# Gates of a hybrid decoder layer: block products in place of plain tiles for ten of twelve pairs of column tiles

## The reference, cut to what matters

```python
gates = jax.nn.sigmoid((h @ w_gate[l] + b_gate[l]).astype(jnp.float32))
gates = gates.astype(x.dtype).reshape(b, s, N_BRANCH, D_MODEL)
merged = (gates[:, :, 0] * (o_a @ w_o_a[l])
          + gates[:, :, 1] * (o_b @ w_o_b[l])
          + gates[:, :, 2] * (o_m @ w_o_m[l]))
x = x + merged @ w_out[l]
x = x + conv_ffn(rmsnorm(x, ffn_norm[l]), w_up[l], conv_w[l], conv_b[l], w_down[l])
```

## Time and profile before

| | |
|---|---|
| time, median of three runs | 1750.19 us (1750.15 to 1750.33) |
| time of the profiled execution | 1753.89 us, of which 1752.1 us are its span |
| PE matmul busy | 1681.4 us (96%) |
| DVE, ACT, POOL busy | 848.1, 634.4, 865.3 us |
| gates stage on PE | 591.05 to 857.29 us of the span |
| output projections | 857.29 to 969.3 us |

### The profile page before, as it was taken

One profiled execution on the slowest core, in us unless ns is written; L12 is line 12 of the kernel. 1 busy time (PEld: TensorE's weight loads), 2 busy tenths in 40 slices (PEclk: granted clock), 3 DMA queues, 4 the chain that ended last, 5 costly groups with the idle time before them and its releaser, 6 DMA issues.

```text
span 1752.1 us, 22400 instructions
## 1 busy us (share of the span) xinstructions
PE 1681.4 (96%) x8625; PEld 1381.5 (79%) x8625; DVE 848.1 (48%) x1242; ACT 634.4 (36%) x1135; POOL 865.3 (49%) x671
## 2 busy tenths in 40 slices
PE   5999999999899899999999999899999999999999
PEld 4887878778677688888888787788888888788887
DVE  6555243457874112200155247788888888522101
ACT  5455565545544222222111323434343334322110
POOL 6543656533322122222144566999999998222221
PEclk9999999999999799999999999999999999999999
DMA  6113011110110233332355711222232223443411
GB/s 214 37 58 100 1 37 40 37 45 13 43 37 1 61 111 97 96 97 84 116 166 165 247 51 48 90 79 73 84 95 74 73 84 101 164 144 132 144 48 60
DMA packets 131253, 151.05 MB, mean 86 GB/s; under 512 B 16780, under 2 KB 97356, under 8 KB 131148
## 3 DMA queue, kind: packets, MB, share of 16 engines
q1 hardware_dynamic: 131148, 149.63, 26.9%
HBM read 116.98 MB, written 32.62 MB: 85 GB/s over the span
## 4 chain that ended last, share of the span: by engine, by line
PE 61%; DVE 2%; POOL 2%; DMA 1%; ACT 1%; issue 0%; SPq 0%; DVEq 0%; ACTq 0%; POOLq 0%
PE ps L2341 23%; PE ps L1694 15%; PE ps L2426 13%; PE ps L1710 6%; PE ps L1726 3%; DMA w_raw<-in_w_out_dram 1%; POOL wo L1587 1%; POOL f_lo L2182 0%; PE ps L1719 0%; DVE ffn_area L2299 0%; DVE attn_lo L2291 0%; DVE t_all L2209 0%; ACT wo L1518 0%; DVE ffn_area L1679 0%; DVE attn_out L2244 0%
## 5 line engine op out<-in xcount | busy, mean ns | idle before, releaser
L2182 POOL TENSOR_TENSOR f_lo<-ffn_area,f_hi 128x1024 fp32r<-128x1024 f32 x85 | 201.8, 2394 | 20.5 <-ACT f_hi L2069 20.5
L2341 PE MATMUL ps<-t_all,f_hi 128*128 128x512 f32 x528 | 164.1, 392 | 2.0 <-DVE t_all L2209 1.6
L1592 POOL TENSOR_TENSOR g_lo<-g_raw,g_hi 128x1024 fp32r<-128x1024 f32 x23 | 55.3, 2406 | 208.5 <-ACT g_hi L1502 208.5
L1694 PE MATMUL ps<-act_hi,g_hi 128*128 128x512 f32 x384 | 152.4, 397 | 3.4 <-DVE g_lo L1627 3.4
L2214 POOL TENSOR_TENSOR attn_lo<-ffn_area,attn_lo 128x512 fp32r<-128x512 f32 x44 | 58.6, 1331 | 194.3 <-ACT attn_lo L2131 194.3
L1694 PE MATMUL ps<-act_hi,g_lo 128*128 128x512 f32 x384 | 151.3, 394 | 0.0
L1694 PE MATMUL ps<-act_lo,g_hi 128*128 128x512 f32 x384 | 150.0, 391 | 0.0
L2069 ACT ACTIVATE f_hi<-ffn_area 128x1024 fp32r<-128x1024 f32 x85 | 80.2, 946 | 187.9 <-PE ps L2341 177.5
L2341 PE MATMUL ps<-act_hi,f_hi 128*128 128x512 f32 x336 | 133.1, 396 | 4.6 <-POOL f_lo L2182 4.6
L2341 PE MATMUL ps<-act_hi,f_lo 128*128 128x512 f32 x336 | 132.5, 394 | 0.0
L1229 PE MATMUL ps<-w_hi,act_hi 128*128 128x512 f32 (+1 forms) x320 | 123.0, 384 | 9.2 <-DVE act_lo L476 4.1
(11 more groups left out here) (258 smaller groups left out, 4257.8 us busy)
## 6 DMA issues: line engine op xcount, KB each, us to landing
ffn_area<-in_w_up_dram SPq DMA_DIRECT2D x44, 512.0 KB, 5.2
gates<-gate SPq DMA_DIRECT2D x24, 512.0 KB, 3.1
gate<-gates SPq DMA_DIRECT2D x24, 512.0 KB, 3.9
g_raw<-in_w_gate_dram SPq DMA_DIRECT2D x23, 512.0 KB, 4.6
z<-attn_out SPq DMA_DIRECT2D x22, 512.0 KB, 2.6
ffn_area<-in_w_down_dram SPq DMA_DIRECT2D x22, 512.0 KB, 4.2
ffn_area<-z SPq DMA_DIRECT2D x44, 256.0 KB, 3.0
attn_out<-in_x_dram SPq DMA_DIRECT2D x16, 512.0 KB, 6.0
```

The source lines that it names most:

```text
L1592: pool.tensor_tensor(g_lo[:, n % 3], g_raw[:, n % 2], g_hi[:, n % 3].bitcast(F32), ALU.subtract).then_inc(g_lo_done, 1)
L1694: ins = pe.matmul(ps[:, u % 4, :], w[:, n % 3, k, :], a[:, k, HALF[half]], start=(k == 0 and i == 0), stop=(k == NK - 1 and i == 2))
L2182: pool.tensor_tensor(part_place(p, part, f_lo, first_lo), part_source(p, part), part_place(p, part, f_hi, first_hi).bitcast(F32), ALU.subt ...
L2341: ins = pe.matmul(out, w, a, start=(start and k == 0 and i == 0), stop=(stop and k == 3 and i == 2))
```

## The change

- Column tiles `p` and `p + 12` form pair `p`. Pairs 0 and 1 stay plain (four tiles, 192 matmuls); pairs 2 to 11 are made by seven block products each (840 matmuls).
- The combined activations `T1` to `T4` are made during the plain tiles: DVE makes ten sums of 2048 elements (`difference`) and four low parts (`t_low`, `t4_low`), ACT four casts. `T4` replaces a block of `act_hi`/`act_lo` after the last plain tile.
- The weights go through the feed-forward's buffers: four raw tiles, `f_hi`/`f_lo` of seven slots, with casts on ACT, sums and low parts on POOL.
- Each pair's four quarters of 128 x 512 are summed by DVE into `staged[:, 0:2]`, put through the sigmoid in place by ACT and stored by 256 KB transfers (48 with those of the plain tiles, instead of 24 of 512 KB).
- The attention rows are no longer split in tiles 3 to 12 but in pair 11, the last, since `attn_hi` now shares memory with `t_all`. That pair takes its products in the order P5, P6, P7, P1, P2, P4, P3. The first products of the output projections wait for the rows and for the quarter sums that free their PSUM banks.
- The `w_o` weights of the first tile are loaded during pair 10 into a raw tile of their own; those of the second tile wait for the last sum. The first four casts of `w_out` wait for the end of the gates, not for the output projections.

The core of the diff, with the order of work on ACT, POOL, DVE and PE:

```diff
-WO_SLOT = [1, 2, 7, 8, 9, 10, 3, 4, 5, 6, 11, 12, 13, 14, 15, 0]
+WO_SLOT = [1, 2, 3, 4, 8, 9, 14, 15, 10, 11, 12, 13, 5, 6, 7, 0]
+GATE_AT = (1, 0, 2)
+SPLIT_ROWS = (0, 1, 2, 3, 6, 7, 8, 9, 4, 5)
+SPLIT_NEEDED = (2, 8, 10)
...
+GATE_PAIRS, PLAIN = 12, 2
+LAST_GATES = GATE_PAIRS - 1
+PLAIN_TILES = [(p, e) for p in range(PLAIN) for e in range(2)]
+PLAIN_SLOT = (A11, S3, S1, S3)
...
+def gate_products(p):
+
+    if p == PLAIN:
+        return P1, P2, P6, P5, P7, P4, P3
+    if p == LAST_GATES:
+        return P5, P6, P7, P1, P2, P4, P3
+    return tuple(range(7))
...
+GATE_CASTS = ([(0, 1), (1, 0), (2, "A1"), (1, 1), (2, "A22"), (2, "S12"), (2, "S34")] +
+              [(p, part) for p in range(PLAIN + 1, GATE_PAIRS) for part in ("S12", "A1", "A22", "S34")])
...
+            if n < 4:
+                eng.wait_ge(p_done, len(GATE_ORDER))
+            else:
+                eng.wait_ge(out_summed, UN * (NK - 1) + (2 if n < 6 else 4 if n < 8 else UN))
...
+            load_gate(0)
+            store_quarter(LAST_GATES, C22)
+            store_quarter(LAST_GATES, C11)
+            load_gate(1)
+            store_quarter(LAST_GATES, C21)
+            load_gate(2)
+            store_quarter(LAST_GATES, C12)
             load_o_weights(1)
...
+            cast(0, 1)
+            cast(1, 0)
             act.wait_ge(vectors_in, 32)
-            for n in range(NG):
-                f, b = n // BR, n % BR
-                for half in range(2):
-                    u = 2 * n + half
-                    if half == 0 and f >= 1:
-                        act.wait_ge(gate_out[b], 16 * f)
-                    act.wait_ge(gate_summed, u + 1)
-                    column = b * NK + f
-                    act.activation(gate[:, b, HALF[half]], ps[:, u % 4, :], ACT.Sigmoid,
-                                   bias=bias[:, column:column + 1]).then_inc(gate_done, 1)
-                if n + 3 < NG:
-                    cast_gate_weights(n + 3)
-                if SPLIT_FROM <= n < SPLIT_FROM + AT:
-                    i = n - SPLIT_FROM
-                    act.activation(attn_hi[:, i, :], attn_out[:, i, :], ACT.Copy).then_inc(attn_hi_done, 1)
-                if n >= NG - BR:
-                    cast_o_weights(0, n - (NG - BR))
+            plain_gate(0, 0, 0)
+            t_high(0)
+            plain_gate(0, 0, 1)
+            cast(2, "A1")
+            plain_gate(0, 1, 0)
+            t_high(1)
+            plain_gate(0, 1, 1)
+            cast(1, 1)
+            cast(2, "A22")
+            plain_gate(1, 0, 0)
+            plain_gate(1, 0, 1)
+            cast(2, "S12")
+            t_high(2)
+            plain_gate(1, 1, 0)
+            plain_gate(1, 1, 1)
+            t4_high()
+            for p in range(PLAIN, LAST_GATES):
+                cast(p, "S34")
+                if p > PLAIN:
+                    quarter_gate(p - 1, C12)
+                first_copy(p)
+                cast(p + 1, "S12")
+                quarter_gate(p, C11)
+                cast(p + 1, "A1")
+                quarter_gate(p, C22)
+                cast(p + 1, "A22")
+                quarter_gate(p, C21)
+            cast(LAST_GATES, "S34")
+            quarter_gate(LAST_GATES - 1, C12)
+            for i in range(6):
+                split_row(i)
+            cast_o_weights(0, 0)
+            for i in range(6, 8):
+                split_row(i)
+            first_copy(LAST_GATES)
+            for b in range(1, BR):
+                cast_o_weights(0, b)
+            for i in range(8, AT):
+                split_row(i)
+            for n in (C22, C11, C21, C12):
+                quarter_gate(LAST_GATES, n)
...
+            low(0, 1)
+            low(1, 0)
+            low(2, "A1")
+            add_weights(2)
+            low(1, 1)
+            low(2, "A22")
+            low(2, "S12")
+            for p in range(PLAIN, GATE_PAIRS):
+                low(p, "S34")
+                if p < LAST_GATES:
+                    add_weights(p + 1)
+                    for part in ("S12", "A1", "A22"):
+                        low(p + 1, part)
...
-            for i in range(AT):
...
+            def t1_made():
+                (a_hi, a_lo), (b_hi, b_lo) = block_of(0, 1), block_of(0, 0)
+                difference(1, t_raw[:, 0, 1], a_hi.bitcast(F32), b_hi.bitcast(F32))
+                difference(2, t_raw[:, 0, 0], a_lo.bitcast(F32), b_lo.bitcast(F32))
+                dve.wait_ge(comb_made, 2)
+                difference(3, t_raw[:, 0, 1], t_raw[:, 0, 1], t_raw[:, 0, 0], ALU.add)
...
+            def t_low(j):
+                dve.wait_ge(comb_hi, j + 1)
+                if j < 2:
+                    dve.wait_ge(comb_made, (4, 6)[j])
+                dve.tensor_tensor(t_all[:, j, 1], t_raw[:, j, 1], t_all[:, j, 0].bitcast(F32), ALU.subtract).then_inc(comb_lo, 1)
...
+            t1_made()
+            t2_made()
+            t_low(0)
+            t4_made()
+            t_low(1)
+            t3_made()
+            t_low(2)
+            t4_low()
+            for p in range(PLAIN, LAST_GATES):
+                if p > PLAIN:
+                    c12_sum(p - 1)
+                    u2_sum(p)
+                    c11_sum(p)
+                else:
+                    c11_sum(p)
+                    u2_sum(p)
+                u3_u4_sums(p)
+                c22_sum(p)
+                c21_sum(p)
+            c12_sum(LAST_GATES - 1)
+            for i in range(8):
+                split_low(i)
+            u2_sum(LAST_GATES)
+            u3_u4_sums(LAST_GATES)
+            c22_sum(LAST_GATES)
+            c11_sum(LAST_GATES)
+            for i in range(8, AT):
+                split_low(i)
+            c21_sum(LAST_GATES)
+            c12_sum(LAST_GATES)
...
+            def block_product(p, i, slot, hi, lo):
+                gate_bank_free(p, i)
+                for k in range(4):
+                    cols = slice(k * P, k * P + P)
+                    for m, (w, a) in enumerate(((f_hi, hi), (f_hi, lo), (f_lo, hi))):
+                        ins = pe.matmul(gate_bank(p, i), w[:, slot, cols], a[:, k, :], start=(k == 0 and m == 0),
+                                        stop=(k == 3 and m == 2))
+                ins.then_inc(p_done, 1)
...
+            for p in range(PLAIN, GATE_PAIRS):
+                for i in gate_products(p):
+                    pe.wait_ge(w_lo_done, gate_cast(p, PART_OF[i]))
+                    if i in COMBINED:
+                        j = COMBINED[i]
+                        if p == PLAIN:
+                            pe.wait_ge(comb_lo, j + 1)
+                        block_product(p, i, SLOT_OF[i], t_all[:, j, 0], t_all[:, j, 1])
+                    else:
+                        if p == PLAIN and i == P4:
+                            pe.wait_ge(comb_lo, 4)
+                        block_product(p, i, SLOT_OF[i], *block_of(*BLOCK_OF[i]))
...
+                    if f == 0:
+                        pe.wait_ge(attn_lo_done, SPLIT_NEEDED[b])
...
+                        elif at < 3:
+                            pe.wait_ge(summed, gate_sum(LAST_GATES, (C11, C21, C12)[at]))
```

More of the change, by code:

```diff
@@ new lines, in gate_sums @@
+def gate_sums(p):
+    if p == PLAIN:
+        return C11, U2, U3, U4, C22, C21, C12
+    if p == LAST_GATES:
+        return U2, U3, U4, C22, C11, C21, C12
+    return U2, C11, U3, U4, C22, C21, C12
+GATE_ORDER = ([(t, h) for t in PLAIN_TILES for h in range(2)] +
+              [(p, i) for p in range(PLAIN, GATE_PAIRS) for i in gate_products(p)])
+GATE_SUMS = [(p, n) for p in range(PLAIN, GATE_PAIRS) for n in gate_sums(p)]
+GATE_CASTS = ([(0, 1), (1, 0), (2, "A1"), (1, 1), (2, "A22"), (2, "S12"), (2, "S34")] +
+              [(p, part) for p in range(PLAIN + 1, GATE_PAIRS) for part in ("S12", "A1", "A22", "S34")])
@@ new lines, in part_place, with gate_bank, quarter, o_source @@
+        def part_place(p, part, w):
+            if part in (0, 1):
+                a = PLAIN_SLOT[PLAIN_TILES.index((p, part))]
+                b = a + 1
+            else:
+                a, b = PLACE[part]
+            return w[:, a:b + 1, :].rearrange("p a n -> p (a n)")
+        def gate_bank(p, i):
+            return ps[:, gate_product(p, i) % 8, :]
+        def quarter(n):
+            e, half = divmod(GATE_STORES.index(n), 2)
+            return quarters[:, e, HALF[half]]
+        def o_source(f):
+            return o_first if f == 0 else o_raw
@@ new lines, in u2_sum, with c11_sum @@
+            def u2_sum(p):
+                dve.wait_ge(copied, p - PLAIN + 1)
+                product_done(p, P6)
+                if p == PLAIN:
+                    dve.wait_ge(gate_out[3], 16 * PLAIN)
+                dve.tensor_tensor(u2, gate_bank(p, P6), s1(p), ALU.add).then_inc(summed, 1)
+            def c11_sum(p):
+                dve.wait_ge(copied, p - PLAIN + 1)
+                product_done(p, P2)
+                quarter_free(p, C11)
+                dve.tensor_tensor(quarter(C11), gate_bank(p, P2), s1(p), ALU.add).then_inc(summed, 1)
```

(30 more changed lines are left out.)

359 lines of the change are left out of this document (263 added, 96 removed).

## The result

The changed kernel takes **1723.42 us** (median of four runs, 1718.7 to 1724.15) against 1750.17 before: a ratio of 0.985, 95% interval 0.9837 to 0.9864, so 24 to 28.5 us less. A second comparison in five rounds gave 1720.33 against 1748.26, 0.9836 (0.9822 to 0.9849). The forecast was 1724.5 us, 25.7 less.

What follows compares the result with a forecast made beforehand. PE's matmul count was taken to bound the stage. Terms: −26.9 on PE, +0.6 and +0.6 us for two stalls, so −25.7 from the median 1750.2 gives 1724.5 us; range for 8 in 10, 1722.6 to 1730.

Steps and rivals of the forecast that it cites:

- PE alone: Gates: 20 plain tiles go (219.7 us), ten pairs of seven products come (192.8 us), a gain of 26.9 us.
- No waits in the steady pairs: Pairs 3 to 11: no stalls, with POOL at 13.7 us of work in a pair of 19.28 us.
- The A1 part: Tightest supply in the steady pairs: its low part ends near 16.1 us, the next pair begins at 19.3.
- The plain tiles: DVE and POOL queue in turns: pair 1's second tile gets its low part at 35.4 us plus about 0.1, against 35.6.
- POOL's third operation: Plain tiles: must be ready before 15.5 us or DVE gets in one operation more; its cast ends at 15.2, margin 0.2.
- a turn lost: Rival: one DVE operation more ahead of pair 1's second-tile low part adds 2.14 us, two 4.3: 1726.0 to 1730; chance 0.20.
- the 0.6: Stall of PE at the second tile of pair 1, taken as 0.6 us with 0 and 2.2 as ends.
- when PE wants the part: Second tile of pair 1: low part needed when six halves are done, 35.6 us after the first matmul.
- DVE's operation of 2048: Plain tiles: 2.29 us by the skill's formula, 2.14 us by the rows with turns, which the sum used.
- The hand-over: Last pair to output projections: PE waits 0.6 us for sum C21, ends 0 and 3; late rival 1727 to 1737, chance 0.06.
- every row meeting POOL: Last pair: ten DVE low parts each 1.44 us longer would make the stall about 12 us.
- `w_out` and the feed-forward stages: Behind the last pair: looser waits of the first `w_out` casts give nothing; everything later moves by the same amount.

Runs made afterwards that it cites:

- thin products: Changed kernel with 9 of 12 matmuls left out of P7, then of P7 and P3, in pairs 3 to 10: ten pairs 177.1 us, then 167.7 us.
- the variants: Five edits of the changed kernel with its code up to the pairs; with its own three traces, eight traces, low part ready at 35.45 or 37.63 us.
- old `w_out` waits: Changed kernel with the casts of `w_out` waiting as in the kernel before: the `w_out` stretch took 109.3 us, as with the new waits.
- C21 first: Changed kernel with DVE making sums C21 and C12 ahead of the last attention row's low part: pairs 192.6 us, no PE wait entering the output projections.
- P7 thin: Changed kernel with 9 of the 12 matmuls of P7 left out in pairs 3 to 10: ten pairs 177.1 us, no PE wait in them.

## Why the prediction was right, and where it was off

- **PE alone:** 26.9 us forecast. The ten pairs took 192.6 against 192.8 forecast; putting 120 matmuls back costs 27.2. Right, and the reason is shown.
- **No waits in the steady pairs:** right. The A1 part was forecast ready at 16.1 us; the thin products put the supply's pace at 16.3. The margin of 3.2 us was right to 0.2.
- **The plain tiles:** the sum of ten DVE and eight POOL holds put the low part at 35.4 us after the first matmul, plus 0.1, or one turn of 2.14 later. PE got it at 35.45 and at 37.63: both values were right to 0.1. The place where the turn is lost was the second one named, POOL's third operation, wanted before 15.5 us; the border lay at 15.42. So the rival "a turn lost" is what the profiled run did, and it happened in two of three traces of this kernel, three of eight with the variants. It was given 0.20. The time still fell into the forecast, since the forecast allowed both stalls up to 2 us together; the 0.6 itself was a mean of two ends, and none of the eight traces shows it.
- **What I had missed there:** when PE wants the part was put at 35.6 us, from one trace. It was 34.4 to 35.9, mostly by how long the clock stays at the lower level at the start, 2.9 to 5.7 us in these traces. So a third outcome came that two ends, 0 and 2.2, leave out: with the turn won and a short stretch, three runs (old `w_out` waits, C21 first, P7 thin) still waited 0.8 to 0.9 us.
- **DVE's operation of 2048:** 2.28 us alone, in line with the 2.29 of the Trainium skill (VectorE: DVE Perf Modes, section "The TRN2 errata — SBUF-src ops pay a fixed extra latency per instruction"). In turns it holds the port for about 2.1 to 2.2, since part of its length overlaps with POOL's. The turns were the right measure for the queue.
- **The hand-over:** 0.6 forecast, 0.6 measured by the matmuls' distances (0.4 in the list of waits), for the sum named, and gone when the sum goes first. A side sum there is off: with every row meeting POOL the forecast's own terms give 13.1 us (3.9 + 25.9 + 3.3 + 0.7 − 20.7) and not 12; nothing hangs on it.
- **`w_out` and the feed-forward stages:** no change forecast, none found once the kernel before had three traces.
- **The total:** −25.7 forecast for the changed stages, −24.1 found there. Of the 1.6 us between them the stall is 0.8 (it cost 2.1, 2.3 and 0 us, 1.4 on the mean of three traces, against 0.6), and 0.6 is the kernel before, whose gates were put at 266.2 from one trace and took 265.6 on the mean of three. The median came out 1.1 us lower than forecast, from the spread of other stages and not from a better account: that the total is so near is in part luck.

## What to carry to other kernels

When a loop is bound by matmuls and another stage of the same kernel already runs the shorter form, that stage's period from the trace is the best price, and the question is only the entry and the exit of the loop. Where DVE and GpSimd both read two operands from SBUF, add their times as one queue, and look for places where two requests come within 0.2 us: such a sum has two values, a turn apart, and a mean between them is no forecast. Give the time at which PE wants the part a range too, when its clock has just been at the lower level. Put the operation that the matmuls wait for ahead of those that have time, even where the sum says that it is just in time. And take more than one trace of the kernel before, ere a difference outside the edited stages is explained.

## What the runs showed of the hardware

- At the start of the gates, after about 3.4 us without a matmul, PE ran at a granted clock of 0.50, its lower level of 1.2 GHz, in every trace. The same program was at it for 4.9 us in one trace and 3.2 in another; over all traces it was 2.9 to 5.7 us. It costs a little under half its length, since matmuls follow each other at 0.43 us in it and at 0.23 behind it:

```profile
591.05:595.90 4.85, 4.85 (x11) 3.79 (x12) 0.00 (x0) 0.18 (x1) 0.00 (x0) 0.50 0.92 189
```

```profile
587.60:590.80 3.20, 3.18 (x8) 2.51 (x9) 0.00 (x0) 0.00 (x0) 0.00 (x0) 0.50 0.85 107
590.80:592.00 1.20, 1.20 (x7) 0.99 (x6) 0.00 (x0) 0.00 (x0) 0.00 (x0) 0.99 1.13 338
```

(Kernel before, first and second trace, columns as above.) The first of them had been at 0.50 since 579 us, while PE still did the last matmuls of the attention part; the second was still at 1.00 from 584 to 587 us. What sets the length of the stretch is not shown.

- The output projections take 110.9 us or 112.0 for the same 480 matmuls and no wait, with records of 393 or 397 ns on the mean for `attn_hi` by `o_hi`. Nothing here tells why.
- The turns of the two engines on the port go by who comes first. POOL's record starts 0.11 us ahead of DVE's in one trace and POOL went first (603.23, 603.34); it starts 0.14 behind in another and DVE went first (603.51, 603.37). The Trainium skill (SBUF — State Buffer, section "Who interferes with whom") says that issue order decides; by that rule, these traces agree. Nearer than 0.02 us the starts of the records no longer tell: POOL's was 0.02 ahead in the third trace of the changed kernel and won, 0.01 ahead in the second (604.19, 604.20) and lost.
